# Two matmuls instead of three for the split products of the up projections

## The chip, the cores and the metric

The kernel runs on one core of one Trainium2 chip. The metric is the device time of one execution, in microseconds; the median of several executions stands for a kernel. One more execution is recorded by the hardware profiler, and all durations in the text come from it.

## The reference

Two transformer blocks over one sequence of 256 tokens with 2048 channels, everything in float32.

```python
# first block: mixer, then the gated feed-forward
u2 = rmsnorm(h, norm_ffn_g)
up = centred_dwconv3(u2 @ ffn_w_up, ffn_conv_w) + ffn_conv_b    # 2048 -> 2 * 5632
a, gv = up[..., :5632], up[..., 5632:]
h = h + (silu(a) * gv) @ ffn_w_down                             # 5632 -> 2048
...
# second block: convolution and window attention, then 16384 experts of width 1
x = x + peer(rms_norm(x, norm2_g), ...)
# peer: per token 8 heads choose 16 experts each, with gates
#   h = x . peer_u[e];  a = gelu(h) * gate;  y = sum over chosen e of a * peer_v[e]
```

The kernel computes the experts densely: all 16384 products `x . peer_u[e]`, gelu, a gate that is zero where an expert isn't chosen, and the product with `peer_v`.

## The kernel before

Float32 accuracy comes from split operands. Weights and inputs are each written as a high part, rounded to the matmul's type (float32r), and a low part, the remainder. A product is the sum of three matmuls into the same PSUM region: high by high, high by low, low by high.

Weights stream through SBUF in units of 128 partitions x 1024 elements (512 KB), 1096 in all, in a fixed list (`units`, filled by `add_units`). `prepare` (line 267) issues a unit's transfer into one of five RAW buffers, then ScalarE writes HI (line 280) and VectorE writes LO = RAW - HI (line 281), into four buffers each. It runs three units ahead of the matmuls (`LOOK`); a HI or LO buffer is written again when the matmuls of the unit four before it are done. So in the order of ScalarE's and VectorE's work the preparation of unit i+3 stands ahead of whatever is put there after the matmuls of unit i.

`product` (line 333) makes one group of 512 output columns for all 256 tokens, over `nk` blocks of 128 contraction rows, two blocks in each unit. It has two forms:
- by token (lines 355 to 357): the input is stationary, 128 tokens of it; 512 weight columns move. 12 matmuls a unit. Used for the down products.
- by channel (lines 365 to 367): 128 weight columns are stationary, the 256 tokens of the input move. 24 matmuls a unit: for each of 4 channel tiles and 2 blocks HI by XH, HI by XL, LO by XH. Used for the up products. XH and XL are two SBUF tiles of 128 x 16 blocks x 256.

The result of a group lies in a pair of PSUM banks; two pairs alternate, and `acc_free[pair]` holds what must have read a pair before it is written again. After each unit `step` is called: it advances one generator of `evacuations`, one of `beside`, and those of `background` at a set rate. This is how other work gets its places in the engines' lists, which each engine works down in order. At the fourth unit of a product `settle` empties `evacuations`.

The feed-forward goes in thirds of 4, 4 and 3 steps of 512 channels. A step is two products of 8 units: the `a` part into AV and the `gv` part into GV. `centred` (line 742) takes them out of PSUM: for each half (one bank) two ScalarE instructions (line 749) and four VectorE taps (lines 648 and 650). Then come silu, or the multiplication (line 769) and the split into FH and FL (`split`, lines 455 and 456), two `step`s later. A third ends with four down products by token over its FH and FL, added to the residual (line 725).

The experts go in 8 chunks of 2048: up, gelu, multiplication with the gates (`weighted`, line 1185), split into FH and FL, down. `up_staged` writes gelu's result to a buffer for chunks 0, 1 and 2, whose gates aren't there yet; `up` with `hidden` (line 1191) does the rest. The gates are built beside it by `gates`, background work of VectorE (lines 1139 to 1145), TensorE (line 1164, 24 small bfloat16 matmuls a block) and ScalarE (line 1173).

Of the kernel before, what the change touches and what calls it, by code (L numbers as in the profile page):

```python
# [8 lines left out]
F32R = mybir.dt.float32r  # L9
# [3 lines left out]
ALU = mybir.AluOpType  # L13
ACT = mybir.ActivationFunctionType
# [3 lines left out]
S = 256  # L18
EPS = 1e-6
NRAW = 5  # L20
NHI = 4
LOOK = 3


CONSTS = {}
# [84 lines left out]
def _program(nc, a, out, ctx):  # L110
# [3 lines left out]
    PE, DV, AC, PO, SP = [Engine(sem("s_" + n)) for n in ("pe", "dve", "act", "pool", "sp")]  # L114
# [4 lines left out]
    def at(name, shape, dt=F32, offset=None):  # L119
        size = 4 * int(np.prod(shape[1:]))  # L120
        if offset is None:
            offset = base[0]
            base[0] += (size + 31) // 32 * 32
            assert base[0] <= 229344, (name, base[0])
        return nc.alloc_sbuf_tensor_at(name, shape, dt, offset=offset)

    const_at = base[0]
# [11 lines left out]
    RAW = at("RAW", [128, NRAW, 1024])  # L139
    HI = at("HI", [128, NHI, 1024], F32R)  # L140
    LO = at("LO", [128, NHI, 1024], F32R)
    XH = at("XH", [128, 16, S], F32R)
    XL = at("XL", [128, 16, S], F32R)
    STAGE = at("STAGE", [128, 16, S], offset=base[0])
    FH = at("FH", [128, 16, S], F32R)
    FL = at("FL", [128, 16, S], F32R)
# [2 lines left out]
    def over(name, shape, where, dt=F32):  # L149
        return at(name, shape, dt, offset=arena + where)  # L150
# [7 lines left out]
    AV = [over(f"AV{i}", [128, 4, S], 4 * K * i) for i in range(2)]  # L158
    GV = [over(f"GV{i}", [128, 4, S], 8 * K + 4 * K * i) for i in range(2)]
    GB1 = over("GB1", [128, D], 16 * K)  # L160
    QT2 = QT
    KT2 = over("KT2", [128, 2, S], 8 * K)
    V2 = over("V2", [128, 2, 128], 10 * K)
# [19 lines left out]
    TG = at("TG", [128, 128, 3, 2], BF16, offset=gb_at + 4 * K)  # L183
    TR = at("TR", [128, 2, S], offset=gb_at + 6 * K)
    mask1_at = const_at + 4 * CONSTS["mask1"][0]
    TAB = at("TAB", [128, 2, S], BF16, offset=mask1_at)
    KEYS2 = at("KEYS2", [128, 128, 2], BF16, offset=mask1_at + K)

# [41 lines left out]
    def add_units(name, groups, width=512):  # L230
        w = a[name]
        for g in groups:
            for u in range(w.shape[1]):
                units.append((w[g, u], 2 * width))

    add_units("w_in", [6, 7, 8, 2, 4, 0, 3, 5, 1, 9, 10, 11, 12])
    add_units("w_out_a", range(4))
# [4 lines left out]
    thirds = [range(0, 4), range(4, 8), range(8, 11)]  # L242
    for th in thirds:
        for q in th:
            add_units("ffn_w_up", [q, 11 + q])
        for g in range(4):
            for u in range(2 * th[0], 2 * th[-1] + 2):
                units.append((a["ffn_w_down"][g, u], 1024))
# [8 lines left out]
    order = [("up", 0), ("up", 1), ("down", 1), ("down", 0)] + [(d, c) for c in range(2, 8) for d in ("up", "down")]  # L257
    for way, c in order:
        if way == "up":
            add_units("peer_ut", range(4 * c, 4 * c + 4))  # L260
            continue
        for g in range(4):
            units.extend((a["peer_v"][g, 8 * c + u], 1024) for u in range(8))
# [69 lines left out]
    def product(by_token, nk, xh, xl, ready, k0=0, width=512):  # L333


        pair = groups[0] % 2
        groups[0] += 1
        banks = [bank(2 * pair), bank(2 * pair + 1)]
        for u in range(nk // 2):
            if u == 3:  # L340
                settle()
            i = len(mm_done)
            prepare(i + LOOK)
            hi = HI[:, i % NHI, 0:2 * width].rearrange("p (k n) -> p k n", k=2)
            lo = LO[:, i % NHI, 0:2 * width].rearrange("p (k n) -> p k n", k=2)
            first, last = u == 0, u == nk // 2 - 1

            def fn(e, u=u, hi=hi, lo=lo, first=first, last=last):
                if by_token:
                    for t in range(2):  # L350
                        o = banks[t][:, 0:width]
                        for k in range(2):
                            x, y = (z[:, k0 + 2 * u + k, 128 * t:128 * t + 128] for z in (xh, xl))
                            f, l = first and k == 0, last and k == 1
                            e.matmul(o, x, hi[:, k, :], start=f, stop=False, skip_group_check=True)  # L355
                            e.matmul(o, x, lo[:, k, :], start=False, stop=False, skip_group_check=True)  # L356
# [12 lines left out]

            mm_done.append(PE.do(fn, hi_done[i], lo_done[i], acc_free[pair] if first else None,  # L370
                                 ready(k0 + 2 * u + 1)))
            step()
        return pair, banks, mm_done[-1]

    t_next = [0]
    t_free = [None] * 4
# [82 lines left out]
    def two(b):  # L459
        return b.rearrange("p (c s) -> p c s", c=2)  # L460
# [278 lines left out]
    un_free.append(m_un_read)  # L739
    m_gb1 = SP.dma(lambda e: e.dma_start(GB1[:], rows(a["norms"][3])), l_gb1, mix_ready)  # L740

    def centred(pair, dst, banks, c0, m, free, then):

        marks = []
        acc_free[pair] = marks
        for b in range(2):
            srcs = [(c, two(banks[b])[:, c % 2, :]) for c in (2 * b, 2 * b + 1)]
            for c, src in srcs:
                m1 = AC.do(lambda e, c=c, src=src: e.activation(dst[:, c, :], src, ACT.Identity,
                                                                bias=par("fb", c0 + c),  # L750
                                                                scale=par("fw", 3 * (c0 + c) + 1)), m, free)
            marks += [taps(dst[:, c, :], src, "fw", c0 + c, m1) for c, src in srcs]
            yield
        then(marks)

    ff_free = [mix_ready, mix_ready]
    m_down = m_y_read
    n_ff = 0
    for n, th in enumerate(thirds):
        act_ready = []  # L760
        for q in th:
            av, gv = AV[n_ff % 2], GV[n_ff % 2]
            silu = []

            def first(m, av=av, silu=silu):
                silu.append(AC.do(lambda e: e.activation(av[:], av[:], ACT.Silu), m))

            def second(m, av=av, gv=gv, silu=silu, j=4 * (q - th[0]), i=n_ff % 2, act_ready=act_ready, m_down=m_down):
                m = DV.do(lambda e: e.tensor_tensor(gv[:], gv[:], av[:], ALU.mult), m, silu[0])
                ff_free[i] = split(FH[:, j:j + 4, :], FL[:, j:j + 4, :], gv[:], m, m_down)  # L770
                act_ready.append(ff_free[i])

            pair, banks, m = product(False, 16, XH, XL, x_ready)
            evacuations.append(centred(pair, av, banks, 4 * q, m, ff_free[n_ff % 2], first))
            pair, banks, m = product(False, 16, XH, XL, x_ready)
            evacuations.append(centred(pair, gv, banks, 44 + 4 * q, m, ff_free[n_ff % 2], second))
            n_ff += 1
        for g in range(4):
            pair, banks, m = product(True, 4 * len(th), FH, FL, lambda k: act_ready[k // 4])
            acc_free[pair] = residual(banks, m, g, n == 2, m_un)  # L780
        m_down = mm_done[-1]
# [404 lines left out]
        gm_read[c % 3].append(m)  # L1186
        return split(FH[:, 4 * j:4 * j + 4, :], FL[:, 4 * j:4 * j + 4, :], dst, m, free[2 * j], free[2 * j + 1])

    def hidden(pair, banks, m, c, j, free, act_ready):
        nonlocal hb_free  # L1190
        acc_free[pair] = m1 = [AC.do(lambda e, i=i: e.activation(HB[:, 2 * i:2 * i + 2, :], two(banks[i]), ACT.Gelu),
                                     m, hb_free) for i in range(2)]
        yield
        hb_free = weighted(c, j, m1, HB[:], HB[:], free)
        act_ready.append(hb_free)

    def up(c, free, act_ready):
        for j in range(4):
            pair, banks, m = product(False, 16, XH, XL, x_ready)
            evacuations.append(hidden(pair, banks, m, c, j, free, act_ready))  # L1200

    def up_staged(dst, staged, free):

# [63 lines left out]
    background.append(gates(1, 2))  # L1267
    free = down(0, ready[0])
    background.append(weigh(2, staged[2], GM[1], free, ready[2]))
    up_staged(GM[1], staged[2], gm_read[1])  # L1270
    flush()
    for m in ready[2]:
        gm_read[1].extend(m)
# [29 lines left out]
        PE.run(e)  # L1303


def _units(w, width=512):

    k, n = w.shape
    return np.ascontiguousarray(w.reshape(k // 256, 2, 128, n // width, width).transpose(3, 0, 2, 1, 4)).reshape(
        n // width, k // 256, 128, 2 * width)  # L1310


def _columns_of(v):
# [49 lines left out]
```

How the kernel before makes its waits and increments, by code:

```python
    def wait(self, *marks):  # L74
        for m in marks:
            if m is None:
                continue
            if isinstance(m, list):
                self.wait(*m)
                continue
            sem, value = m
            if self.passed.get(id(sem), 0) < value:
                self.passed[id(sem)] = value
                self.queue.append(lambda e, sem=sem, value=value: e.wait_ge(sem, value))
# [1 line left out]
    def do(self, fn, *marks):  # L86
        self.wait(*marks)
        self.n += 1
        self.queue.append(lambda e: fn(e).then_inc(self.sem, 1))
        return (self.sem, self.n)
# [1 line left out]
    def dma(self, fn, landing, *marks):  # L92
        self.wait(*marks)
        landing[1] += 16
        self.queue.append(lambda e: fn(e).then_inc(landing[0], 16))
        return (landing[0], landing[1])
```

## Time and profile before

| | |
|---|---|
| median of 3 runs | 3514.8 us (3513.61 to 3515.14) |
| the profiled execution | 3517.23 us |
| its span, first to last instruction | 3515.4 us |
| mean granted TensorE clock | 0.981 |
| matmuls | 24778, busy 3350.9 us (95%) |
| VectorE busy | 2123.7 us (60%) |
| ScalarE busy | 1551.9 us (44%) |
| read from HBM | 584.96 MB, 167 GB/s over the span |

PE stands for TensorE's matmuls, PEld for its weight loads, DVE for VectorE, ACT for ScalarE, SP for the engine that issues the transfers. Matmuls overlap, so the duration of one is longer than the time from its start to the next one's; it is the latter, the pitch, that counts in a dense stretch. Up stages and down stages alternate in the feed-forward (648 to 1471 us, to its last down product) and in the experts (from about 1890 us on).

### The profile page before, as it was taken

The page shows a single profiled execution, that of the slowest core. Times are in us where ns is not written, and L with a number is a line of the kernel's source. Part 1 is how long each engine was busy: PE and PEld are TensorE (multiplying, and loading weights), DVE is VectorE, ACT ScalarE, POOL GpSimd, SP SyncE. Part 2 cuts the span into 40 slices and gives each one's busy share as a digit, 9 for nine tenths or more (in the row PEclk, how much of TensorE's full clock was granted, in tenths as well). Part 3 has the DMA queues.
Part 4 walks back from the last instruction along what each step waited for, and adds up shares of the span by engine and source line. Part 5 has one row for each costly group of instructions (what it writes and reads, how often), then busy time and mean ns, then how long its engine had stood idle before and what let it go on. Part 6 is the DMA issues. An engine that isn't in the chain of part 4 may idle for free.

```text
span 3515.4 us, 60015 instructions
## 1 busy us (share of the span) xinstructions
PE 3350.9 (95%) x24778; PEld 3083.8 (88%) x24778; DVE 2123.7 (60%) x2862; ACT 1551.9 (44%) x2018; POOL 3.5 (0%) x10
## 2 busy tenths in 40 slices
PE   7999999999999998887988889999999999999999
PEld 6999998899999997786778888889898998989897
DVE  5664445656466565675359986676666556655544
ACT  4554444444444444456443334434444443434343
POOL 0000000000000000000000000000000000000000
PEclk9999999999999999898999999999999999999999
DMA  6545655555655655431254443554555555555655
GB/s 213 168 152 185 208 183 177 182 184 188 188 184 187 191 182 167 138 128 60 90 171 134 133 137 129 193 177 159 179 169 174 182 183 171 172 180 183 194 181 167
DMA packets 161135, 590.97 MB, mean 168 GB/s; under 512 B 17888, under 2 KB 17920, under 8 KB 159584
## 3 DMA queue, kind: packets, MB, share of 16 engines
q1 hardware_dynamic: 160624, 586.69, 51.5%
q8 instruction: 198, 3.24, 0.4%
q0 software_dynamic: 240, 0.44, 0.1%
q14 instruction: 73, 0.60, 0.1%
HBM read 584.96 MB, written 2.10 MB: 167 GB/s over the span
## 4 chain that ended last, share of the span: by engine, by line
PE 87%; DVE 10%; ACT 2%; issue 1%; DMA 0%; SPq 0%; DVEq 0%; ACTq 0%
PE PS L365 15%; PE PS L366 15%; PE PS L367 15%; PE PS L355 12%; PE PS L357 12%; PE PS L356 12%; DVE LO L281 3%; PE PS L1164 2%; PE PS L911 2%; DVE GB L882 1%; DVE TK L998 1%; DVE TK L1001 1%; PE PS L579 0%; DVE TK L1000 0%; DMA GB<-in_norms 0%
## 5 line engine op out<-in xcount | busy, mean ns | idle before, releaser
L281 DVE TENSOR_TENSOR LO<-RAW,HI 128x1024 fp32r<-128x1024 f32 (+1 forms) x1096 | 1331.5, 1219 | 1065.5 <-ACT HI L280 1059.1
L280 ACT ACTIVATE HI<-RAW 128x1024 fp32r<-128x1024 f32 (+1 forms) x1096 | 1153.0, 1056 | 1401.1 <-PE PS L367 770.8
L365 PE MATMUL PS<-XH,HI 128*128 128x256 f32 x4864 | 1393.3, 286 | 46.2 <-DVE LO L281 29.1
L366 PE MATMUL PS<-XL,HI 128*128 128x256 f32 x4864 | 1381.2, 284 | 0.0
L367 PE MATMUL PS<-XH,LO 128*128 128x256 f32 x4864 | 1380.5, 284 | 0.0
L365 PEld LDWEIGHTS PS<-XH,HI 128*128 128x128 f32 x4864 | 938.4, 193 | 57.4 <-issue 47.7
L366 PEld LDWEIGHTS PS<-XL,HI 128*128 128x128 f32 x4864 | 939.1, 193 | 0.3
L367 PEld LDWEIGHTS PS<-XH,LO 128*128 128x128 f32 x4864 | 938.4, 193 | 0.0
L355 PE MATMUL PS<-HI,FH 128*128 128x512 f32 x1504 | 593.9, 395 | 19.7 <-DVE FL L456 16.2
L357 PE MATMUL PS<-HI,FL 128*128 128x512 f32 x1504 | 587.0, 390 | 0.0
L356 PE MATMUL PS<-LO,FH 128*128 128x512 f32 x1504 | 586.4, 390 | 0.0
L355 PEld LDWEIGHTS PS<-HI,FH 128*128 128x128 f32 x1504 | 283.1, 188 | 77.6 <-DVE FL L456 11.0
L357 PEld LDWEIGHTS PS<-HI,FL 128*128 128x128 f32 x1504 | 283.1, 188 | 61.0
L356 PEld LDWEIGHTS PS<-LO,FH 128*128 128x128 f32 x1504 | 283.4, 188 | 57.2
L1139 DVE TENSOR_TENSOR OH<-KEYS,TAB 128x1024 bf16<-128x1024 bf16 x128 | 88.5, 691 | 90.9 <-PE PS L1164 90.8
L355 PE MATMUL PS<-HI,XH 128*128 128x512 f32 (+1 forms) x320 | 123.8, 387 | 6.9 <-DVE XL L456 3.9
L356 PE MATMUL PS<-LO,XH 128*128 128x512 f32 (+1 forms) x320 | 123.2, 385 | 0.0
L357 PE MATMUL PS<-HI,XL 128*128 128x512 f32 (+1 forms) x320 | 123.0, 385 | 0.0
L1164 PEld LDWEIGHTS PS<-GOH,OH 128*128 128x128 bf16 x3072 | 85.0, 97 | 18.2 <-issue 14.1
L1164 PE MATMUL PS<-GOH,OH 128*128 128x32 bf16 x3072 | 97.3, 177 | 0.0
L725 DVE TENSOR_TENSOR RES<-PS,RES 128x512 f32<-128x512 f32 x112 | 72.1, 686 | 24.7 <-PE PS L357 24.7
L355 PEld LDWEIGHTS PS<-HI,XH 128*128 128x128 f32 x320 | 61.5, 192 | 19.2 <-ACT XH L455 4.1
(224 smaller groups left out, 1923.3 us busy)
## 6 DMA issues: line engine op xcount, KB each, us to landing
RAW<-in_peer_ut SPq DMA_DIRECT2D x256, 512.0 KB, 3.6
RAW<-in_peer_v SPq DMA_DIRECT2D x256, 512.0 KB, 3.6
RAW<-in_ffn_w_up SPq DMA_DIRECT2D x176, 512.0 KB, 4.2
RAW<-in_w_in SPq DMA_DIRECT2D x136, 512.0 KB, 4.1
RAW<-in_ffn_w_down SPq DMA_DIRECT2D x88, 512.0 KB, 4.2
RAW<-in_w_mix_out SPq DMA_DIRECT2D x32, 512.0 KB, 4.1
RAW<-in_w_in_2c SPq DMA_DIRECT2D x32, 512.0 KB, 3.6
RAW<-in_w_out SPq DMA_DIRECT2D x32, 512.0 KB, 3.6
```

Source lines behind the costliest of these rows:

```text
L280: hi_done.append(AC.do(lambda e, raw=raw, hi=hi: e.activation(hi, raw, ACT.Copy), landed[i], used))
L281: lo_done.append(DV.do(lambda e, raw=raw, hi=hi, lo=lo: e.tensor_tensor(lo, raw, hi.bitcast(F32), ALU.subtract), hi_done[i], landed[i], used))
L355: e.matmul(o, x, hi[:, k, :], start=f, stop=False, skip_group_check=True)
L356: e.matmul(o, x, lo[:, k, :], start=False, stop=False, skip_group_check=True)
L357: m = e.matmul(o, y, hi[:, k, :], start=False, stop=l, skip_group_check=True)
L365: e.matmul(o, h, x, start=f, stop=False, skip_group_check=True)
L366: e.matmul(o, h, y, start=False, stop=False, skip_group_check=True)
L367: m = e.matmul(o, w, x, start=False, stop=l, skip_group_check=True)
L725: r = DV.do(lambda e, d=d, b=banks[t]: e.tensor_tensor(d, b, d, ALU.add), m, *more)
L911: dg_read[n] = m = PE.do(lambda e, k=k, n=n: e.matmul(b[:, 0:S], DG[:, n, :], HP[:, c, k:k + S], start=k == 0, stop=k == 30, skip_group_ch ...
L1139: m_oh = DV.do(lambda e: e.tensor_tensor(OH2[:, k], KEYS2[:].unsqueeze(1).to_broadcast([128, 4, 128, 2]), pairs(1, 128), ALU.is_equal), m_ ...
L1164: m = e.matmul(o, OH2[:, k, j // 2, :, j % 2], GOH[:, k, j // 2, i, :, j % 2], start=i == 0, stop=i == 2, skip_group_check=True)
```

## The change

High and low input are put side by side, block by block, in one tile XX; XH and XL become views of it. A new function `product_both` makes 256 output columns at a time, one bank for each of its two channel tiles. For each tile and block one matmul of 512 columns takes HI by (XH, XL), so that the bank's first half collects high by high and its second half high by low; a second matmul of 256 columns adds LO by XH to the first half. At the end ScalarE copies the second halves to SBUF (BF or BP), and VectorE adds them to the first halves and writes the sum to its destination. This copy and this add are issued inside `product_both`, ahead of its last `step`. `settle` is called at the third of its four units.

It is used for the feed-forward's up products, where the sum goes to a new buffer ZF that `centred` reads, and for the up products of expert chunks 2 to 7, where it goes to HB or to the stage's buffer and gelu works on it in place. The other products, those of chunks 0 and 1 among them, stay as they were. The weights of the changed products are cut on the host into units of 4 blocks x 256 columns instead of 2 x 512; their size and number stay.

```diff
-    XH = at("XH", [128, 16, S], F32R)
-    XL = at("XL", [128, 16, S], F32R)
+    XX = at("XX", [128, 16, 2, S], F32R)
+    XH, XL = XX[:, :, 0, :], XX[:, :, 1, :]
...
+    ZF = [over(f"ZF{i}", [128, 4, S], 24 * K + 4 * K * i) for i in range(2)]
+    BF = over("BF", [128, 2, S], 32 * K)
...
+    BP = at("BP", [128, 2, S], offset=const_at + 4 * CONSTS["mask2"][0])
...
-            add_units("ffn_w_up", [q, 11 + q])
+            add_units("ffn_w_up", [2 * q, 2 * q + 1, 22 + 2 * q, 23 + 2 * q])
...
+            if c < 2:
+                add_units("peer_ut", range(4 * c, 4 * c + 4))
+            else:
+                add_units("peer_ut_rest", range(8 * (c - 2), 8 * (c - 2) + 8))
...
+    sum_free = {}
+
+    def product_both(ready, dst, rest, free):
+
+
+        pair = groups[0] % 2
+        groups[0] += 1
+        halves = PS[:, 1024 * pair:1024 * pair + 1024].rearrange("p (c h s) -> p c h s", c=2, h=2)
+        for u in range(4):
+            if u == 2:
+                settle()
+            i = len(mm_done)
+            prepare(i + LOOK)
+            hi = HI[:, i % NHI, :].rearrange("p (k n) -> p k n", k=4)
+            lo = LO[:, i % NHI, :].rearrange("p (k n) -> p k n", k=4)
+
+            def fn(e, u=u, hi=hi, lo=lo):
+                for c in range(2):
+                    o = bank(2 * pair + c)
+                    w = slice(128 * c, 128 * c + 128)
+                    for k in range(4):
+                        x = XX[:, 4 * u + k, :, :].rearrange("p h s -> p (h s)")
+                        e.matmul(o, hi[:, k, w], x, start=u == 0 and k == 0, stop=False, skip_group_check=True)
+                        m = e.matmul(o[:, 0:S], lo[:, k, w], x[:, 0:S], start=False, stop=u == 3 and k == 3,
+                                     skip_group_check=True)
+                return m
+
+            mm_done.append(PE.do(fn, hi_done[i], lo_done[i], acc_free[pair] if u == 0 else None, ready(4 * u + 3)))
+            if u < 3:
+                step()
+        m = mm_done[-1]
+        m_rest = AC.do(lambda e: e.activation(rest[:], halves[:, :, 1, :], ACT.Copy), m, sum_free.get(id(rest)))
+        acc_free[pair] = sum_free[id(rest)] = m_sum = DV.do(lambda e: e.tensor_tensor(
+            dst, halves[:, :, 0, :], rest[:], ALU.add), m, m_rest, free())
+        step()
+        return m_sum
...
-            pair, banks, m = product(False, 16, XH, XL, x_ready)
-            evacuations.append(centred(pair, av, banks, 4 * q, m, ff_free[n_ff % 2], first))
-            pair, banks, m = product(False, 16, XH, XL, x_ready)
-            evacuations.append(centred(pair, gv, banks, 44 + 4 * q, m, ff_free[n_ff % 2], second))
+            for i, (dst, c0, then) in enumerate(((av, 4 * q, first), (gv, 44 + 4 * q, second))):
+                z, marks = ZF[i], []
+                ms = [product_both(x_ready, z[:, 2 * b:2 * b + 2, :], BF, lambda i=i: zf_free[i]) for b in range(2)]
+                zf_free[i] = marks
+                evacuations.append(centred(dst, z, c0, ms, ff_free[n_ff % 2], marks, then))
...
     def up(c, free, act_ready):
         for j in range(4):
-            pair, banks, m = product(False, 16, XH, XL, x_ready)
-            evacuations.append(hidden(pair, banks, m, c, j, free, act_ready))
+            ms = [product_both(x_ready, HB[:, 2 * i:2 * i + 2, :], BP, lambda: hb_free) for i in range(2)]
+            evacuations.append(hidden(c, j, ms, free, act_ready))
...
-    up_staged(GM[1], staged[2], gm_read[1])
+    up_staged_both(GM[1], staged[2], gm_read[1])
...
-        "ffn_w_up": _units(g["ffn_w_up"][0]),
+        "ffn_w_up": _units(g["ffn_w_up"][0], 256, 4),
...
-        "peer_ut": _units(g["peer_u_2"].T),
+        "peer_ut": _units(g["peer_u_2"][:4096].T),
+        "peer_ut_rest": _units(g["peer_u_2"][4096:].T, 256, 4),
```

## Rows read from the trace of the kernel before

**Rows 1.** The page: the span, busy times, and the chain that ended last.
```profile
span 3515.4 us, 60015 instructions
PE 3350.9 (95%) x24778; PEld 3083.8 (88%) x24778; DVE 2123.7 (60%) x2862; ACT 1551.9 (44%) x2018; POOL 3.5 (0%) x10
...
PE 87%; DVE 10%; ACT 2%; issue 1%; DMA 0%; SPq 0%; DVEq 0%; ACTq 0%
```

**Rows 2.** The windows view by stage: window, length, busy us and count, clock, DMA.
```profile
core 0: us, PE busy (x) PEld busy (x) DVE busy (x) ACT busy (x) POOL busy (x), PEclk, DMA share, GB/s
832.20:919.20 87.00, 87.00 (x386) 72.05 (x385) 48.30 (x48) 36.59 (x37) 0.00 (x0) 1.00 0.62 193
919.30:1103.50 184.20, 184.20 (x1536) 184.19 (x1535) 109.48 (x128) 87.75 (x99) 0.00 (x0) 1.00 0.57 184
...
2377.60:2480.70 103.10, 102.75 (x1129) 101.91 (x1128) 65.04 (x79) 43.84 (x57) 0.00 (x0) 1.00 0.48 155
...
2576.00:2675.80 99.80, 99.80 (x1037) 99.33 (x1034) 63.76 (x76) 42.47 (x53) 0.00 (x0) 1.00 0.53 169
...
3331.50:3423.50 92.00, 92.00 (x769) 92.00 (x768) 46.99 (x40) 39.74 (x41) 0.00 (x0) 1.00 0.59 184
```

**Rows 3.** The timeline of PE at stage seams: start us, us, what.
```profile
832.24 0.40 PE L355 MATMUL PS<-HI,FH 128*128 128x512 f32 x1
...
919.08 0.39 PE L357 MATMUL PS<-HI,FL 128*128 128x512 f32 x1
919.31 0.28 PE L365 MATMUL PS<-XH,HI 128*128 128x256 f32 x1
919.42 0.28 PE L366 MATMUL PS<-XL,HI 128*128 128x256 f32 x1
...
1103.50 0.28 PE L367 MATMUL PS<-XH,LO 128*128 128x256 f32 x1
```

**Rows 4.** Groups by line and shape: busy us, mean ns; last a DMA issue.
```profile
L281 DVE TENSOR_TENSOR LO<-RAW,HI 128x1024 fp32r<-128x1024 f32 x1088 | 1326.0, 1223 | 1057.6 <-ACT HI L280 1051.2
L280 ACT ACTIVATE HI<-RAW 128x1024 fp32r<-128x1024 f32 x1088 | 1147.9, 1059 | 1389.7 <-PE PS L367 770.8 <-PE PS L357 617.7
...
L365 PEld LDWEIGHTS PS<-XH,HI 128*128 128x128 f32 x4864 | 938.4, 193 | 57.4 <-issue 47.7 <-ACT HI L280 6.1 <-ACT UN L528 1.3
...
L725 DVE TENSOR_TENSOR RES<-PS,RES 128x512 f32<-128x512 f32 x112 | 72.1, 686 | 24.7 <-PE PS L357 24.7
...
L446 ACT ACTIVATE XH<-PS 128x512 fp32r<-128x512 f32 x32 | 19.1, 598 | 23.8 <-PE PS L440 23.4
...
RAW<-in_ffn_w_up SPq DMA_DIRECT2D x176, 512.0 KB, 4.2
```

**Rows 5.** The timeline of DVE, then ACT, behind a feed-forward step's second product.
```profile
698.32 1.21 DVE L281 TENSOR_TENSOR LO<-RAW,HI 128x1024 fp32r<-128x1024 f32 x1
...
701.27 1.22 DVE L281 TENSOR_TENSOR LO<-RAW,HI 128x1024 fp32r<-128x1024 f32 x1
702.40 1.22 DVE L769 TENSOR_TENSOR GV<-GV,AV 128x1024 f32<-128x1024 f32 x1
704.75 1.23 DVE L456 TENSOR_TENSOR FL<-GV,FH 128x1024 fp32r<-128x1024 f32 x1 [1.12 <-ACT FH L455]
...
697.14 1.06 ACT L280 ACTIVATE HI<-RAW 128x1024 fp32r<-128x1024 f32 x1 [0.91 <-PE PS L367]
...
703.66 1.06 ACT L455 ACTIVATE FH<-GV 128x1024 fp32r<-128x1024 f32 x1 [2.58 <-DVE GV L769]
```

**Rows 6.** The timelines at the start of the three-step down stage: DVE, PE.
```profile
1339.67 1.22 DVE L456 TENSOR_TENSOR FL<-GV,FH 128x1024 fp32r<-128x1024 f32 x1 [1.13 <-ACT FH L455]
...
1328.92 0.40 PE L355 MATMUL PS<-HI,FH 128*128 128x512 f32 x1
...
1341.04 0.47 PE L355 MATMUL PS<-HI,FH 128*128 128x512 f32 x1 [1.05 <-DVE FL L456]
```

**Rows 7.** The timelines late in chunk 2's up stage: DVE, PE.
```profile
2463.70 1.23 DVE L1185 TENSOR_TENSOR GM<-GM,GM 128x1024 f32<-128x1024 f32 x1 [1.80 <-ACT UN L1173]
...
2476.44 4.62 DVE L281 TENSOR_TENSOR LO<-RAW,HI 128x1024 fp32r<-128x1024 f32 x4
...
2477.80 0.35 PE L365 MATMUL PS<-XH,HI 128*128 128x256 f32 x1 [0.35 <-DVE LO L281]
```

More of the change, by code:

```diff
@@ L233, in add_units @@
             for u in range(w.shape[1]):
-                units.append((w[g, u], 2 * width))
+                units.append((w[g, u], w.shape[3]))
     add_units("w_in", [6, 7, 8, 2, 4, 0, 3, 5, 1, 9, 10, 11, 12])
@@ L259, in _program @@
         if way == "up":
-            add_units("peer_ut", range(4 * c, 4 * c + 4))
+            if c < 2:
+                add_units("peer_ut", range(4 * c, 4 * c + 4))
+            else:
+                add_units("peer_ut_rest", range(8 * (c - 2), 8 * (c - 2) + 8))
             continue
@@ L740, in _program, with centred @@
     m_gb1 = SP.dma(lambda e: e.dma_start(GB1[:], rows(a["norms"][3])), l_gb1, mix_ready)
-    def centred(pair, dst, banks, c0, m, free, then):
-        marks = []
-        acc_free[pair] = marks
+    def centred(dst, z, c0, ms, free, marks, then):
         for b in range(2):
-            srcs = [(c, two(banks[b])[:, c % 2, :]) for c in (2 * b, 2 * b + 1)]
+            srcs = [(c, z[:, c, :]) for c in (2 * b, 2 * b + 1)]
+            m = ms[b]
             for c, src in srcs:
@@ L756, in _program @@
     ff_free = [mix_ready, mix_ready]
+    zf_free = [mix_ready, mix_ready]
+    sum_free[id(BF)] = mix_ready
     m_down = m_y_read
@@ L1187, in weighted, with gelu, hidden @@
         return split(FH[:, 4 * j:4 * j + 4, :], FL[:, 4 * j:4 * j + 4, :], dst, m, free[2 * j], free[2 * j + 1])
-    def hidden(pair, banks, m, c, j, free, act_ready):
+    def gelu(d, m):
+        return AC.do(lambda e: e.activation(d, d, ACT.Gelu), m)
+    def hidden(c, j, ms, free, act_ready):
         nonlocal hb_free
-        acc_free[pair] = m1 = [AC.do(lambda e, i=i: e.activation(HB[:, 2 * i:2 * i + 2, :], two(banks[i]), ACT.Gelu),
-                                     m, hb_free) for i in range(2)]
+        m1 = [gelu(HB[:, 2 * i:2 * i + 2, :], ms[i]) for i in range(2)]
         yield
@@ L1198, in up, with up_staged_both @@
         for j in range(4):
-            pair, banks, m = product(False, 16, XH, XL, x_ready)
-            evacuations.append(hidden(pair, banks, m, c, j, free, act_ready))
+            ms = [product_both(x_ready, HB[:, 2 * i:2 * i + 2, :], BP, lambda: hb_free) for i in range(2)]
+            evacuations.append(hidden(c, j, ms, free, act_ready))
+    def up_staged_both(dst, staged, free):
+        for j in range(4):
+            blocks = [dst[:, 4 * j + 2 * i:4 * j + 2 * i + 2, :] for i in range(2)]
+            ms = [product_both(x_ready, b, BP, lambda: free) for b in blocks]
+            staged.append([gelu(b, m) for b, m in zip(blocks, ms)])
     def up_staged(dst, staged, free):
@@ L1303, in _, with _units @@
         PE.run(e)
-def _units(w, width=512):
+def _units(w, width=512, tiles=2):
     k, n = w.shape
-    return np.ascontiguousarray(w.reshape(k // 256, 2, 128, n // width, width).transpose(3, 0, 2, 1, 4)).reshape(
-        n // width, k // 256, 128, 2 * width)
+    u = k // (128 * tiles)
+    return np.ascontiguousarray(w.reshape(u, tiles, 128, n // width, width).transpose(3, 0, 2, 1, 4)).reshape(
+        n // width, u, 128, tiles * width)
 def _columns_of(v):
```

## The prediction

> **What bounds the kernel now.** I read the page first: TensorE's matmuls are busy for 3350.9 of 3515.4 us, VectorE for 60% and ScalarE for 44%, and in the chain that ended last 87% is PE [rows 1]. A busy share alone doesn't say that TensorE is at its pace, so I cut the span into stages with the windows view. In the feed-forward's up stages and in the expert up stages without gate work PE and PEld are both busy for the whole window, at a granted clock of 1.00 (2.4 GHz), while VectorE works 109.5 of 184.2 us and DMA is at 0.57 to 0.59 [rows 2]. Then the timeline for the pitch, start to start. From 919.31 to 1103.50 there are 1535 steps between 1536 matmuls of 256 columns: 120.0 ns each. From 832.24 to 919.08 there are 383 steps between 384 matmuls of 512 columns: 226.7 ns each [rows 3]; the counts are those of the windows, less the neighbours at their edges [rows 2]. These averages run over 64 and 32 units, so the switch from one unit to the next costs nothing more, and no wait is in them. The difference, 106.7 ns for 256 more columns, is one column per cycle at 2.4 GHz. Both widths thus carry the same surplus: 120.0 - 106.7 = 13.3 ns and 226.7 - 213.3 = 13.4 ns for each matmul with its weight load, whatever its width.
>
> **The change, part by part.** *The products.* Today one pair (block of 128 contraction rows, 128 output channels) takes three matmuls of 256 columns: high weights by high input, high by low, low by high, 3 x 120.0 = 360.0 ns. Afterwards it takes one of 512 and one of 256: 226.7 + 120.0 = 346.7 ns. The columns are the same 768; one load and one surplus go: 13.3 ns. A unit has 8 such pairs in the old cut (2 blocks x 4 channel tiles) and in the new one (4 blocks x 2), and holds 512 KB either way. Units that change: 176 of the feed-forward (22 groups x 8) and 192 of experts 4096 to 16383 (6 chunks x 4 groups x 8), 368 in all, 2944 pairs. 2944 x 13.26 ns = **39.0 us less**. All of this lies on the path, since PE is the bound in these stages: 99.8 of 99.8 us also in an up stage with gate work beside it, 102.75 of 103.1 in the first changed expert stage [rows 2].
>
> The trace of before doesn't show the two widths in turn for long. It shows the seam: the last 512 starts at 919.08, the first 256 at 919.31, the next at 919.42 [rows 3], so 0.23 and 0.11 us, as in each form by itself. From above the pair is bounded by three matmuls at 120.0 (360.0, if the surplus doesn't go) and from below by 226.7 + 106.7 = 333.4 (if the 256 finds its weights already in and loses its surplus too). I take 346.7, the sum of the two rows, because the seam is the nearest row. The ends give 0 and 78.3 us saved.
>
> The Trainium skill (TensorE: Matmul & The Clock Gate, Back-to-back issue gap) gives a warm gap of columns over 2.4 GHz plus about 2.5 ns. The rows show a surplus of 13.3 ns, five times that, in a stream where every matmul has a load of its own. By the page's figure the removed matmul would be worth 2.5 x 2944 = 7 us, an estimate, against 39 by the rows; here the row decides.
>
> *The sums.* Each half product (92 of them, 368 / 4) ends with a ScalarE copy of 128x512 out of PSUM (0.60 us by the row of line 446) and a VectorE add of 128x512 with one operand in PSUM (0.69 us by line 725) [rows 4]. That is 92 x 0.69 = 63 us more on VectorE and 55 on ScalarE. In a feed-forward stage VectorE goes from 109.5 to about 120.5 of 177.5 us; with gates from 64 to about 69 of 96.5. Neither becomes the bound by its load.
>
> What matters is the order, since both engines work strictly down their lists. Copy and add are put right behind the product's last unit i (end: T), ahead of the next preparation. Behind the copy stands line 280's HI of unit i+4, which had to wait for T anyway. By durations (HI 1.06, LO 1.22) [rows 4]: copy to T+0.6, add to T+1.35, HI to T+1.7, LO to T+2.9, and PE wants that unit three units later, at T+8.3. Cover 5.4 us, so nothing at an ordinary boundary. PSUM comes free at T+1.35, wanted again at T+11.
>
> The tightest ordinary place is the end of the feed-forward's second product, 11 times. Now [rows 5], with T = 694.3 (the HI at 697.14 is released by unit i+1, one unit of 2.88 after it), these start: LO of i+5 at T+4.0, LO of i+6 at T+7.0 (behind the second set of taps), multiplication at T+8.1, FH at T+9.4, FL at T+10.5. Afterwards the taps start 0.65 later (add plus launch), so the second set ends at T+7.7; and `settle` is at the third unit, ahead of its preparation, so that multiplication (to 8.8), FH (to 9.95) and FL (to 11.2) come before LO of i+6. That LO ends at T+12.4; PE wants it at T + 5 x 2.77 = T+13.9. Cover 1.5 us, so the cost is between 0 and 11 x 1.35 = 15 us (at that end the cover is gone and another copy and add fall in); I take 0.
>
> *Two places without cover.* The last up product before the three-group down stage: there PE already waits 1.05 us for FL [rows 6], because the last step's blocks are wanted four units after the stage begins. FL comes 0.55 us later: **+0.6 us**. And the first changed expert stage: late in it VectorE and ScalarE turn three blocks in a chain that started at 2463.70, a burst of four LO follows at 2476.44, and PE waits 0.35 us for the first [rows 7]. The half product's add (+0.65) falls into that chain, and PE arrives 5 units x 0.107 = 0.53 us earlier, counted from the last gate matmul: **+1.2 us**. In the other down stages the last block is wanted at their seventh unit, T+16.3, and FL is there by T+12.5: nothing.
>
> *The rest, at nothing.* Transfers keep their size and number and land in 4.2 us [rows 4]; a unit every 2.77 us asks for less than the down stages already get (2.72 us, 193 GB/s) [rows 2]. Steps per unit stay the same, so gates and other background work keep their places. The input's blocks lie 2 KB apart instead of 1 KB, which alters no element count. Reading Z from SBUF in place of PSUM is off PE's path.
>
> Sum for the profiled span: 3515.4 - 39.0 + 0.6 + 1.2 = 3478.2, and with the 1.8 us around it 3480.0 against 3517.23. That execution was 2.4 us over the median of the runs shown (3514.8), so the prediction is 3514.8 - 37.2 = **3477.6 us**.
>
> **Rivals.** *A, a new wait of TensorE for LO:* the order above misses its 1.5 us of cover at the 11 feed-forward boundaries, and somewhat at those with gates. Price up to 15 us: 3492. For it: three engines in strict order and PE 4% faster; against it: covers of 1.5 and 5.4 us counted from rows. *B, the surplus stays:* it belongs to something that is still there (the change of high and low weights, say), the pair costs 360.0, and only the 1.8 us (less for PE's pace) is added: 3516. Against it: 384 matmuls of 512 and 1536 of 256 in the same order of high and low show the same 13.3 ns each. *C, slower:* in the alternation the load of the next high weights isn't pulled ahead any more. A PEld takes 193 ns [rows 4] and the matmul above it only 120, so up to 73 ns per pair would stand open: 346.7 + 73 = 420 ns, +60 x 2944 = +177 us, 3692. It decides against the change from 13.3 ns open per pair. Against it: 256-column matmuls hide the same load today and the load of the low weights now lies under 226.7 ns. *D, better:* the 256 finds its weights loaded and costs 106.7: 333.4 ns a pair, 39 us more saved, 3438. Against it: the seam.
>
> **How the numbers follow.** Forecast 0.76, A 0.11, B 0.05, C 0.04, D 0.04. By itself the forecast spans 3474 (neither place costs) to 3483 (each costs three times as much, and a few boundaries slip). The range takes in A: 3470 to 3493; B, C and D are outside, 0.13. A measurement of this kernel can tell about 0.2% (7 us) from none. Faster by more: forecast, A and D, 0.91; within: B, 0.05; slower: C, 0.04.
>
> **What the changed profile would show.** Right: the 512 starting 0.227 us before its 256 and that one 0.120 before the next 512; a feed-forward stage of 64 units lasting 177.5 us in place of 184.3; an expert up stage without gates 88.7 in place of 92.0; about 21,830 matmuls; VectorE near 2187 us, ScalarE near 1607; PE's waits for LO and FL in those stages below 4 us in all. Wrong: any other pitch in the alternation (B, C, D), or idle time of PE before the first matmul of a unit that recurs once per group (A).

## The result: half of the forecast gain

| | before | after |
|---|---|---|
| median | 3514.4 us (4 runs) | 3496.7 us (4 runs, 3494.4 to 3498.3) |
| ratio | | 0.9947 (95%: 0.9935 to 0.9959) |
| profiled execution, its span | 3517.2, 3515.4 us | 3497.5, 3495.8 us |

The change is worth 17.8 us (0.5%), where 37.2 were forecast. 3496.7 lies outside the range, above its end of 3493. The kernel is faster; the size is wrong. The page of the kernel after, as [rows 1, 4] show it for before:

```profile
span 3495.8 us, 54346 instructions
...
PE 3328.6 (95%) x21834; PEld 2921.1 (84%) x21834; DVE 2185.1 (63%) x2954; ACT 1597.4 (46%) x2110; POOL 3.5 (0%) x10
...
PE 86%; DVE 10%; ACT 2%; issue 1%; DMA 1%; SPq 0%; DVEq 0%; ACTq 0%
...
L403 PE MATMUL PS<-XX,HI 128*128 128x512 f32 x2944 | 1045.2, 400 | 1.2 <-DVE LO L287 1.2
L404 PE MATMUL PS<-XX,LO 128*128 128x256 f32 x2944 | 826.6, 281 | 0.0
L403 PEld LDWEIGHTS PS<-XX,HI 128*128 128x128 f32 x2944 | 553.1, 188 | 137.1 <-ACT HI L286 1.5
...
L371 PEld LDWEIGHTS PS<-XX,HI 128*128 128x128 f32 x1920 | 373.6, 195 | 58.3 <-issue 48.9
```

Everything that was counted rather than timed came as forecast: 21834 matmuls, VectorE 2185.1 us (2187 forecast), ScalarE 1597.4 (1607). TensorE waits 1.2 us for LO in all the changed products together. So the time isn't lost in waits. The windows view of three changed stages (the second third of the feed-forward, chunk 2, chunk 7), to be held against [rows 2]:

```profile
912.77:1093.66 180.89, 180.89 (x1025) 156.82 (x1024) 119.55 (x143) 94.38 (x114) 0.00 (x0) 1.00 0.56 187
2367.47:2469.82 102.35, 101.14 (x874) 87.34 (x873) 69.33 (x86) 47.89 (x64) 0.00 (x0) 1.00 0.45 156
3313.52:3403.96 90.44, 90.44 (x514) 78.39 (x512) 51.80 (x47) 43.29 (x48) 0.00 (x0) 1.00 0.55 187
```

TensorE is busy for the whole of the first and the third, at a granted clock of 1.00 as before, and still they last 180.9 us instead of the 177.5 forecast and 90.4 instead of 88.7. That is 2826 ns for a unit of 8 pairs, 353.3 ns a pair; 346.7 was forecast. 2944 pairs x 6.6 ns = 19.4 us, and 37.2 - 19.4 = 17.8: the whole miss is in the pitch. The timeline of PE in chunk 7, at its start and further on (start us, us, what):

```profile
3313.29 0.39 PE L363 MATMUL PS<-HI,FL 128*128 128x512 f32 x1
3313.52 0.39 PE L403 MATMUL PS<-XX,HI 128*128 128x512 f32 x1
3313.74 0.28 PE L404 MATMUL PS<-XX,LO 128*128 128x256 f32 x1
...
3319.87 0.40 PE L403 MATMUL PS<-XX,HI 128*128 128x512 f32 x1
3320.10 0.28 PE L404 MATMUL PS<-XX,LO 128*128 128x256 f32 x1
3320.22 0.40 PE L403 MATMUL PS<-XX,HI 128*128 128x512 f32 x1
3320.45 0.28 PE L404 MATMUL PS<-XX,LO 128*128 128x256 f32 x1
3320.57 0.40 PE L403 MATMUL PS<-XX,HI 128*128 128x512 f32 x1
3320.81 0.28 PE L404 MATMUL PS<-XX,LO 128*128 128x256 f32 x1
3320.93 0.40 PE L403 MATMUL PS<-XX,HI 128*128 128x512 f32 x1
...
3403.96 0.40 PE L361 MATMUL PS<-HI,FH 128*128 128x512 f32 x1
```

From 3313.52 to 3403.96 are 256 pairs: 353.3 ns each. The first 512 of the stage, behind other 512s, takes 0.22 us as at the seam in [rows 3]. Further in, three pairs take 0.35, 0.35 and 0.36 us, and this pattern of three (1.06 us) repeats: 3319.87 to 3320.93. The mean start to start is 236 ns from a 512 to its 256 and 117 ns onwards, in place of 226.7 and 120.0. So the step from a wide matmul behind a narrow one to the next start is longer by 9 ns, and the narrow one's gives back 3.

### The profile page after: what moved, and what is told of

Same layout as the page of the kernel before. It is cut to its first block, busy times and chain, and to the rows that moved or that the text cites. A ratio compares the mean times of both kernels' runs of the same rounds, so it can differ in the third digit from the quotient of the medians.

```text
span 3495.8 us, 54346 instructions
## 1 busy us (share of the span) xinstructions
PE 3328.6 (95%) x21834; PEld 2921.1 (84%) x21834; DVE 2185.1 (63%) x2954; ACT 1597.4 (46%) x2110; POOL 3.5 (0%) x10
## 4 chain that ended last, share of the span: by engine, by line
PE 86%; DVE 10%; ACT 2%; issue 1%; DMA 1%; SPq 0%; DVEq 0%; ACTq 0%
PE PS L403 20%; PE PS L361 12%; PE PS L363 12%; PE PS L362 12%; PE PS L404 10%; PE PS L371 6%; PE PS L372 5%; PE PS L373 5%; DVE LO L287 3%; PE PS L1209 2%; PE PS L956 2%; DVE GB L927 1%; DVE TK L1043 1%; DVE TK L1046 1%; PE PS L622 0%
## 5 line engine op out<-in xcount | busy, mean ns | idle before, releaser
L403 PE MATMUL PS<-XX,HI 128*128 128x512 f32 x2944 | 1045.2, 400 | 1.2 <-DVE LO L287 1.2
L404 PE MATMUL PS<-XX,LO 128*128 128x256 f32 x2944 | 826.6, 281 | 0.0
L403 PEld LDWEIGHTS PS<-XX,HI 128*128 128x128 f32 x2944 | 553.1, 188 | 137.1 <-ACT HI L286 1.5
L371 PE MATMUL PS<-XX,HI 128*128 128x256 f32 x1920 | 557.0, 290 | 47.3 <-DVE LO L287 29.1
L404 PEld LDWEIGHTS PS<-XX,LO 128*128 128x128 f32 x2944 | 556.2, 189 | 0.2
L372 PE MATMUL PS<-XX,HI 128*128 128x256 f32 x1920 | 548.3, 286 | 0.0
L373 PE MATMUL PS<-XX,LO 128*128 128x256 f32 x1920 | 547.5, 285 | 0.0
L371 PEld LDWEIGHTS PS<-XX,HI 128*128 128x128 f32 x1920 | 373.6, 195 | 58.3 <-issue 48.9
L372 PEld LDWEIGHTS PS<-XX,HI 128*128 128x128 f32 x1920 | 373.8, 195 | 0.0
L373 PEld LDWEIGHTS PS<-XX,LO 128*128 128x128 f32 x1920 | 373.5, 195 | 0.0
L361 PE MATMUL PS<-HI,XX 128*128 128x512 f32 (+1 forms) x320 | 122.5, 383 | 6.9 <-DVE XX L499 3.9
L362 PE MATMUL PS<-LO,XX 128*128 128x512 f32 (+1 forms) x320 | 122.5, 383 | 0.0
L363 PE MATMUL PS<-HI,XX 128*128 128x512 f32 (+1 forms) x320 | 122.4, 382 | 0.0
```

The costliest lines, as they stand in the source:

```text
L403: e.matmul(o, hi[:, k, w], x, start=u == 0 and k == 0, stop=False, skip_group_check=True)
L404: m = e.matmul(o[:, 0:S], lo[:, k, w], x[:, 0:S], start=False, stop=u == 3 and k == 3, skip_group_check=True)
```

## Experiments

A unit's time below is that of its stage, from its first matmul to the first of the down stage, over its 64, 48 or 32 units; it is read in the six stages that have no gate products between their matmuls (the feed-forward's three, chunks 4, 6 and 7). Without any extra a unit would take 8 x 346.7 = 2773 ns. The changed kernel's takes 2826, the old one's 2880. The runs `second_half` and `both_512` and the four probes were made once each, so they are read by their stages' pitches and not by small differences of the total.

**Is it the order of widths?** Theory T1: the change of width costs; T2: the wide matmul is slower in this form; T3: the bank is written twice in a row. The same matmuls in another order, inside `product_both`:

```diff
 for c in range(2):                        # tile_runs: 4 wide, 4 narrow
     for k in range(4):
         e.matmul(o, hi[:, k, w], x, ...)
-        e.matmul(o[:, 0:S], lo[:, k, w], x[:, 0:S], ...)
+    for k in range(4):
+        e.matmul(o[:, 0:S], lo[:, k, w], XX[:, 4 * u + k, 0, :], ...)
```

> Within each channel tile of a unit the four 512-column matmuls come first, then the four of 256; same matmuls, same count. The changed kernel's pair takes 353.4 ns, 6.7 more than the 226.7 + 120.0 of the separate forms; 2944 pairs give 19.7 us. Theory T1, the step from a 512 to a narrower 256 costs 6.7 ns each time: two such steps a unit remain in place of eight, 736 in place of 2944, so 14.7 us less than the changed kernel's 3496.7: 3482, with 226.7 inside the runs of 512 and 120.0 inside those of 256. Theory T2, a 512-column matmul over high and low input side by side costs 233.3 by itself (its operand or its place in PSUM): 3497 as the changed kernel, 233.3 inside the runs.

Measured: 3488.0 us, ratio 0.9923 (0.9907 to 0.9940); a unit takes 2806 ns.

With both channel tiles' wide matmuls first, then all narrow ones (8 and 8):

> All eight 512-column matmuls of a unit first (both channel tiles), then all eight of 256: one step from 512 to 256 a unit, 368 in all. T1: 17.2 us less than the changed kernel, 3479.5, within 2 us of what was predicted for the change. T2: 3497.

Measured: 3485.1 us, ratio 0.9916 (0.9900 to 0.9933); a unit takes 2793 ns. Both are faster than the change, so T2 falls: what a wide matmul costs depends on its neighbours. But T1 as written had 3482 and 3479.5. Eight changes a unit cost 53 ns together, two 33, one 19: the price isn't one for each change.

Two more edits of the changed kernel, each a run of its own, leave the order and touch the low weights' matmul alone:

```diff
-  e.matmul(o[:, 0:S], lo[:, k, w], x[:, 0:S], ...)
+  e.matmul(o[:, S:2 * S], lo[:, k, w], x[:, 0:S], ...)       # second_half
...
-  e.matmul(o[:, 0:S], lo[:, k, w], x[:, 0:S], ...)
+  e.matmul(o, lo[:, k, w], x, ...)                           # both_512
```

> The 256-column matmul of the low weights adds to the second half of the bank, where high weights by low input are collected; the final sum is the same. Widths and order are those of the changed kernel. T1: pair 353.4 ns, 3497. Theory T3, the extra time comes from the first half of the bank being written by the 256 right behind the 512 that wrote it: the 512 goes back to 226.7 ns, pair 346.7, 3477.

Measured: 3495.8 us, and 2826 ns a unit in five of the six stages. T3 falls. The sixth, the first third of the feed-forward, is a surprise: 2775 ns, the forecast pitch, from the same instructions as in the other two thirds. The timeline of that stage and of the next:

```profile
699.72 0.39 PE L403 MATMUL PS<-XX,HI 128*128 128x512 f32 x1
...
700.06 0.39 PE L403 MATMUL PS<-XX,HI 128*128 128x512 f32 x1
...
700.41 0.39 PE L403 MATMUL PS<-XX,HI 128*128 128x512 f32 x1
...
700.75 0.39 PE L403 MATMUL PS<-XX,HI 128*128 128x512 f32 x1
...
999.92 0.40 PE L403 MATMUL PS<-XX,HI 128*128 128x512 f32 x1
...
1000.28 0.40 PE L403 MATMUL PS<-XX,HI 128*128 128x512 f32 x1
...
1000.63 0.40 PE L403 MATMUL PS<-XX,HI 128*128 128x512 f32 x1
...
1000.98 0.40 PE L403 MATMUL PS<-XX,HI 128*128 128x512 f32 x1
```

Three pairs take 1.03 us in the first and 1.06 in the second. The alternation has two steady rhythms (in the quick one 230.0 and 116.7 ns, start to start), and which one a stage falls into isn't set by its own order and widths. Of the 18 stages of all runs that alternate the changed kernel's 512 and 256 with no gate products between them, this one alone kept to the quick one. But it isn't foreign to the changed kernel: in its chunks 3 and 5 the second and third unit last 2774 and 2777 ns, until the first gate products come between.

> The low weights meet both halves too, so both matmuls of a pair have 512 columns (low by low, left out so far, is added). T1: no change of width inside a unit, 226.7 + 226.7 = 453.3 ns a pair, 99.9 ns more than the changed kernel's 353.4, 2944 x 99.9 = 294 us more: 3791. T2: 233.3 for each, 466.7 a pair: 3830.

Measured: 3793.6 us and 453.3 ns a pair, as T1 had it. Alternating HI and LO as weights costs nothing by itself, nor does reading the same input twice in a row.

**Is it the rest of the change?** The new structure with the old matmuls:

```diff
-  e.matmul(o, hi[:, k, w], x, ...)
+  e.matmul(o[:, 0:S], hi[:, k, w], xh, ...)
+  e.matmul(o[:, S:2 * S], hi[:, k, w], xl, ...)
   e.matmul(o[:, 0:S], lo[:, k, w], xh, ...)
```

> The changed kernel with its new units, its copy and add and its order of work, but each block again with three matmuls of 256 columns (high by high into the first half of the bank, high by low into the second, low by high into the first). It measures everything of the change except the 512. By the prediction's account this costs 1.8 us (0.6 and 1.2 at the two places without cover, a little less since TensorE isn't faster here): 3515 to 3517, pitch 120.0. If the copies and adds cost more at the group boundaries (rival A), 3520 and above, with waits for LO once a group.

Measured: 3515.7 us against 3515.9 for before on that chip, ratio 1.0001 (0.9992 to 1.0011), 2880 ns a unit, and TensorE waits at the two places foreseen and nowhere else (1.5 us for FL, 0.9 for LO). Copies, adds, sums, layout and new units together cost under 4 us, and rival A is out.

**How the price depends on the run.** Runs joined across units, 16 wide and 16 narrow:

```diff
+  if u % 2:
+      narrow()
+      return wide()
+  wide()
+  return narrow()
```

> As the run with all eight wide matmuls of a unit first, but every second unit starts with its narrow ones, so that runs of equal width join across units: 184 times wide to narrow and back in place of 368. In that run a unit cost 2792.6 ns, 19.3 more than 8 x 346.7. If that is the price of one change of width and back, whatever the length of the runs: 9.6 ns a unit less, 3.6 us: 3481.5. If the price lies in each narrow or wide matmul: no difference, 3485.

Measured: 3482.0 us, ratio 0.9904 (0.9888 to 0.9921), 2783 ns a unit. Halving the number of changes halves the extra, so a run of eight or more pays once, 19 to 20 ns, when it goes wide again. This is the fastest of the kernels here that compute everything, 15 us below the change.

> One look, each stage with another order, read from the pitches of the trace. First third of the feed-forward: as the change, but 512 and 256 of a neighbouring pair go to different PSUM banks; if the extra 6.7 ns come from the shared bank, pair 346.7, if from the change of width, 353.4. Second third: two of 512, then two of 256; between the 353.4 of runs of one and the 350.8 a pair of runs of four. Third third and chunks 2 and 5: as the change, 353.4. Chunks 3 and 4: eight and eight, each matmul on a line of its own, to see which matmul of a run is late: only the first after the change of width, if the change itself costs. Chunk 6: 512 and 384 (the low weights meet half of the low input too): 226.7 + 173.3 = 400.0, more by 6.7 if any difference of width costs. Chunk 7: 512 and 128 (the low weights are left out for half of the tokens): 226.7 + 66.7 = 293.3, the same 6.7 more. In all about 3498 - 0.5 (runs) + 12 (384) - 14 (128): 3495.

Measured: 3499.7 us. Chunk 4 has each of the 8 + 8 matmuls on its own line. One unit of it (wide ones on lines 431 to 445, narrow ones on 447 to 461):

```profile
2753.33 0.28 PE L461 MATMUL PS<-XX,LO 128*128 128x256 f32 x1
2753.45 0.40 PE L431 MATMUL PS<-XX,HI 128*128 128x512 f32 x1
2753.69 0.40 PE L433 MATMUL PS<-XX,HI 128*128 128x512 f32 x1
2753.92 0.39 PE L435 MATMUL PS<-XX,HI 128*128 128x512 f32 x1
...
2754.84 0.39 PE L443 MATMUL PS<-XX,HI 128*128 128x512 f32 x1
2755.07 0.39 PE L445 MATMUL PS<-XX,HI 128*128 128x512 f32 x1
2755.29 0.28 PE L447 MATMUL PS<-XX,LO 128*128 128x256 f32 x1
2755.41 0.28 PE L449 MATMUL PS<-XX,LO 128*128 128x256 f32 x1
```

Over the 32 units the eight wide ones take on average 233, 236, 228, 232, 231, 227, 227 and 227 ns to the next start, the eight narrow ones 113, 119 and then 120 each. So the first narrow matmul behind wide ones is 7 ns *quicker* than in its own stream, and the first five wide ones behind narrow ones take 27 ns more together. T1 had the sign wrong: going narrow gains, going wide pays, for several matmuls. The other stages: two wide and two narrow 2787 ns a unit (under both of the values between which I expected it), neighbouring pairs in different banks 2797, 512 and 384 columns 406.6 ns a pair against 400.0, and 512 and 128 columns 339.8 against the 293.3 expected. The 2797 is a mean over both rhythms: from the third group on, groups of four units last 11.3 and 11.1 us in turn, the slow and the quick one. So the same order in different banks runs at either pitch, and sharing a bank isn't what sets it. The first unit of each group has two wide and two narrow matmuls together, and the groups also alternate between two pairs of banks; which of these tips the rhythm is open. The 512 and 128 are the telling ones: 339.8 - 226.7 = 113 ns for a matmul whose 128 columns take 53. Something other than moving columns sets it. Only the sum can be read in this way, since the records place the time differently: 280.0 ns from a wide start to the narrow one and 60.0 onwards.

> One look, another order in some stages. Third third of the feed-forward: three matmuls of 256 in the new structure, 360.0 for the three. Chunk 4: 384 and 256 (high weights by half of the low input is left out): 173.3 + 120.0 = 293.3 without extra, 300.0 if any change of width costs 6.7. Chunk 6: 512 and 256 with the high weights for both (low weights by high input left out): 353.4 if the width costs, 346.7 if the alternation of the HI and LO tiles does. Chunk 7: 256 and 128 (low input, and the low weights for half of the tokens, left out): 120.0 + 66.7 = 186.7, or 193.4. The other stages as the change, 353.4 a pair; a stage at 346.7, as the first one of the second-half run, may turn up again. In all about 3497 + 1 - 15 - 42: 3441.

Measured: 3453.2 us. Three of 256 columns took 360.0 ns, as expected. With the high weights for both, 353.3 ns: the widths, not the tiles. 384 and 256: 293.3, the value without an extra, though its term for 384 columns (173.3) assumes the same surplus of 13.3 and no run has such a stream by itself. 256 and 128: 237.3 a pair over the stage, where 186.7 or 193.4 was expected. TensorE waits there three times for LO (0.33 to 0.35 us), each time with slower units around; the undisturbed units last 1849 to 1855 ns, 231.5 a pair or 116 a matmul. Again some 115 ns for each matmul with its load, and the 120.0 ns of a 256-column stream lie close to that.

**Is it the weight load?**

```diff
-  (bank(...)[:, a:b],   weights[:, k, 128 * c:128 * c + 128], x[:, a:b])
+  (bank(...)[0:n, a:b], weights[:, k, 128 * c:128 * c + n],   x[:, a:b])    # n = 64
```

> One look; orders and widths of the moving side are those of the change everywhere, but in three expert stages the stationary side is narrower, so its load shorter. The runs so far: pure streams have no extra (226.7, 120.0), the extra falls on the 512-column matmuls that come after 256-column ones, and a unit with eight and eight pays 19 ns on its first five wide ones. Theory L: the load of the next weights hardly fits under a 256-column matmul, so after narrow ones the loads run late and the wide ones pay for it. Then chunk 4, high weights of 64 columns (their load runs under the 256): pair 346.7 or less. Chunk 6, low weights of 64 columns (their load runs under the 512): still 353.3. Chunk 7, both of 64: 346.7 or less. Rival M: the extra lies in the stream of moving columns or in PSUM, not in the loads: 353.3 in all three. Half of the output channels of the products concerned are left out in these chunks (hi in 4 and 7, lo in 6 and 7). In all 3493 by L, 3497 by M.

Measured: 3488.2 us. The timeline of chunk 4 (high weights of 64 columns, line 413), then of chunk 6 (low weights of 64, line 421):

```profile
2759.86 0.39 PE L413 MATMUL PS<-XX,HI 128*64 128x512 f32 x1
2760.09 0.28 PE L415 MATMUL PS<-XX,LO 128*128 128x256 f32 x1
2760.20 0.39 PE L413 MATMUL PS<-XX,HI 128*64 128x512 f32 x1
...
2760.88 0.39 PE L413 MATMUL PS<-XX,HI 128*64 128x512 f32 x1
...
3134.84 0.39 PE L419 MATMUL PS<-XX,HI 128*128 128x512 f32 x1
3135.07 0.28 PE L421 MATMUL PS<-XX,LO 128*64 128x256 f32 x1
3135.19 0.39 PE L419 MATMUL PS<-XX,HI 128*128 128x512 f32 x1
...
3135.89 0.39 PE L419 MATMUL PS<-XX,HI 128*128 128x512 f32 x1
```

340.1 ns a pair in chunks 4 and 7 (227.0 and 113.0), 346.7 in chunk 6. M's 353.3 came in none of the three: the stream of columns is the same, and the extra goes with a narrower stationary side. The part of M that blames PSUM isn't excluded by this, since fewer partitions are written too. L was right for chunks 4 and 7 and wrong for chunk 6, where it had 353.3: shortening the load that lies under the *wide* matmul also removes 6.6 ns. So it isn't simply that one load doesn't fit under the narrow matmul. The two loads of a pair matter together.

> One look. Orders of the same matmuls in the feed-forward: first third, two wide and two narrow, taken over both channel tiles: as the runs of two so far, 2787 ns a unit, if only the order of widths counts. Second third, runs of three (and a last of two): between 3.3 and 16.4 ns extra for each of three changes, 2790 to 2820 a unit. Third third, runs of six and of two: about 2773 + 19 + 3 = 2796. Chunk 4: three matmuls of 256 with weights of 64 columns: 120.0 each if the 13.3 ns over the columns don't depend on the load's length (rival M), about 113 if half a load costs half (L). Chunk 6: two of 512 with weights of 64 columns: 226.7 each by M, 220 by L. Chunk 7: 128 columns each, high weights of 64 and low ones of 128 columns: 66.7 + 13.3 = 80 each if nothing but columns and surplus count, more if the load is longer than that. In chunks 4, 6 and 7 half of the output channels, in 7 also half of the tokens and the low input, are left out. In all about 3497 - 3 - 2 + 26 - 40: 3478.

Measured: 3492.9 us. Orders: 2787 ns a unit for two and two over both tiles (2788 in this first third, which runs 1 to 2 ns a unit over the other two in every kernel here), 2796 for runs of three, and 2780 for six and two, where 2796 was expected. Chunk 4, three of 256 with weights of 64 columns, in the timeline:

```profile
2759.87 0.28 PE L421 MATMUL PS<-XX,HI 128*64 128x256 f32 x1
2759.98 0.28 PE L423 MATMUL PS<-XX,HI 128*64 128x256 f32 x1
...
2760.78 0.28 PE L425 MATMUL PS<-XX,LO 128*64 128x256 f32 x1
```

Its 768 matmuls take 113.3 ns each instead of 120.0. A stream of 256-column matmuls is thus held up by its 128-column weights, by 6.7 ns each. Chunk 6 doesn't fit: two of 512 with 64-column weights take 460.0 ns a pair, more than the 453.3 with 128, and that stays unexplained.

Chunk 7 has two matmuls of 128 columns each, the first with weights of 64 columns and the second with 128. Its mean of 266 ns a pair, where 160 was the least expected, mixes two clocks. The windows view of two parts, and the timeline of PE in the first part and at the wait behind it:

```profile
3330.10:3346.60 16.50, 16.50 (x194) 16.50 (x193) 14.83 (x15) 12.34 (x14) 0.00 (x0) 1.00 0.80 285
3360.00:3398.20 38.20, 38.20 (x241) 38.20 (x240) 25.04 (x23) 20.12 (x23) 0.00 (x0) 0.50 0.67 220
...
3338.00 0.22 PE L435 MATMUL PS<-XX,HI 128*64 128x128 f32 x1
3338.06 0.28 PE L437 MATMUL PS<-XX,LO 128*128 128x128 f32 x1
3338.18 0.22 PE L435 MATMUL PS<-XX,HI 128*64 128x128 f32 x1
...
3350.94 0.24 PE L435 MATMUL PS<-XX,HI 128*64 128x128 f32 x1 [2.82 <-DVE LO L287]
```

At a granted clock of 1.00 the first twelve units take 1373 to 1378 ns each, 171.7 a pair. VectorE, busy 14.83 of 16.50 us, hardly keeps up with such units, and at 3350.94 TensorE has waited 2.82 us for LO; behind this wait the granted clock is 0.50, and a pair takes 320.0 ns to the end of the stage. So the 113 to 116 ns aren't a fixed price of a matmul. At full clock 64 + 128 weight columns took 171.7 ns here, and 128 + 128 took 231.5 in the 256 and 128, both about 0.9 ns for each weight column, while the moving columns would take 107 and 160.

## Why the prediction was wrong

**Right:** what bounds the kernel, the count of pairs, and that the gain lies on the path. The places without cover: 1.52 us of waiting for FL in place of 1.05 (+0.5, forecast +0.6), 1.21 in place of 0.35 in chunk 2 (+0.9, forecast +1.2). No wait at the 11 feed-forward boundaries with their 1.5 us of cover, and none elsewhere: two rows of the timeline of PE, the answers to [rows 6, 7].

```profile
1329.01 0.47 PE L361 MATMUL PS<-HI,FH 128*128 128x512 f32 x1 [1.52 <-DVE FL L499]
...
2466.91 0.47 PE L403 MATMUL PS<-XX,HI 128*128 128x512 f32 x1 [1.21 <-DVE LO L287]
```

**The step that failed** is the pair's price, "346.7, the sum of the two rows, because the seam is the nearest row". It measured 353.3. Three things were wrong in it.

First, the sum. The equal surplus of 13.3 ns at both widths was read as a constant of each matmul. By the runs the two are unlike. A 256-column matmul with 64-column weights takes 113.3 ns, 6.7 over its columns, and weights of 128 columns add the other 6.7. A 512-column matmul among its kind is 13.3 over its columns with 128-column weights (226.7), and weights of 64 columns don't lower that (230.0 in the last probe). A pitch that hangs on the weights around it is a property of the stream, not of the instruction, and can't be carried into another stream unchecked.

The trace of before had a hint, though a weak one. Weight loads last 193 ns in the 256-column stream [rows 4] and, in the page's row for the 512-column one, 188; after the change they are 188 in the alternation and 195 in what is left of the old stream (the page above). That the longer ones wait for something is a guess, and in the alternation, which does pay, their duration shows nothing. The Trainium skill (TensorE: Matmul & The Clock Gate, LDWEIGHTS (loading the stationary operand)) puts a load at its columns over 1.2 GHz, 106.7 ns for 128. The 113 and 116 ns per matmul in the two probes lie 6 and 9 ns above that figure; had I set it beside the 120.0, the tightness would have been plain. The prediction's rival C did name the load under the narrow matmul, but allowed it only as a gap of up to 73 ns a pair, and was set aside because "256-column matmuls hide the same load today". They don't quite: with 64-column weights that stream is 6.7 ns a matmul quicker.

Second, the seam. It shows one 512 followed by a 256, and that is the direction that costs nothing: the changed kernel's own seam shows 0.22 us too. The price lies in the way back, and the trace of before has that as well, at the end of each dense up stage. The timeline of PE behind the last row of [rows 3], in the kernel before:

```profile
1103.62 0.40 PE L355 MATMUL PS<-HI,FH 128*128 128x512 f32 x1
1103.86 0.40 PE L356 MATMUL PS<-LO,FH 128*128 128x512 f32 x1
...
1104.55 0.39 PE L356 MATMUL PS<-LO,FH 128*128 128x512 f32 x1
```

From 1103.62 to 1104.55 four wide matmuls take 0.93 us, 232.5 ns each where 226.7 is the pitch: the same longer steps that the probe's chunk 4 shows behind its narrow eight. All nine seams of that trace from an up stage of 256 columns into a down stage, where TensorE doesn't wait, show the same steps: 233 or 234, 235 or 236, 228 or 229, 232 or 233 and 231 ns, then 226 or 227. That is 27 ns a seam, which a mean over 384 matmuls hides; less the 8 that a seam in the other direction gains, it is the 19 ns that a unit with eight and eight pays. I had looked at one direction only.

Third, the range. The prediction itself gave 333.4 and 360.0 ns as bounds of a pair, and then let the range hold only the sum's value and rival A. Between those bounds lie 78 us; a pair at 353.3 is well inside. Rival B asked whether the surplus stays, all or nothing. Half of it stayed.

**What is shown and what is only argued.** Shown: the extra comes with the mixture of 512 and 256 columns and not with the rest of the change; it stands behind the starts of wide matmuls that follow narrow ones; it comes to 53, 13, 23, 33 and 19 ns a unit for runs of one, two, three (the last one of two), four and eight; it falls with a narrower stationary side, and with it the pitch of the 256-column stream falls as well. Argued: that it is the *load* of that side, which the 0.9 ns for each weight column speak for (a narrower stationary side also gives fewer output partitions, and no run parts the two). Open: why runs of two cost less than runs of four, why 512 columns with 64-column weights aren't quicker, and what picks the rhythm. Nor is it known whether 384 columns pay, as their own stream wasn't measured. Over its moving columns alone a pair costs 26.7 ns in the quick rhythm, in 384 with 256 and in 512 with 512, and 33.3 in the slow rhythm and in 512 with 384, so the two rhythms' values turn up there again.

## What to carry to other kernels

Before adding up pitches from two streams, ask for each what limits it: where a stream gets quicker with a narrower stationary side (here 256 columns, 113.3 ns for 120.0), its pitch isn't its moving columns' own, and the bounds of the new mixture belong in the range. If wide and narrow matmuls must be mixed, put equal widths together in long runs: that alone was worth 15 us here, nearly as much as the change itself (18). And when a mean over a seam decides, look at the step in both directions.

## What the runs showed of the hardware

- Short matmuls took longer than their moving columns: with weights of 128 columns a pair of 512 and 128 columns took 339.8 ns and one of 256 and 128 took 231.5; two of 128 columns with weights of 64 and 128 took 171.7, and 320.0 at a granted clock of 0.50.
- Start to start at a granted clock of 1.00 (2.4 GHz): 512 columns 226.7 ns, 256 columns 120.0 with loads of 128 columns and 113.3 with loads of 64.
- Behind narrow matmuls the first five of 512 columns take 233, 236, 228, 232 and 231 ns; the first of 256 behind wide ones takes 113.
- The same alternation of 512 and 256 has two steady rhythms: 353.3 ns a pair in five stages of the kernel that used the bank's second half, and 346.9 in the sixth, for 178 us on end.
